# Eight rolling-cache rows to a partition on 96 and 32 neighbouring partitions, in one attention stage

## The reference, cut to what matters

```
DIL_PATTERNS = ((128, 1), (512, 4), (2048, 16))
kc = jnp.concatenate([cache_win_k[i], kb], axis=1)      # (8, 2048 + 8, 8, 64)
vc = jnp.concatenate([cache_win_v[i], vb], axis=1)
...
idx = w + arange(n_new)[:, None] - dil * arange(n_back + 1)[None, :]   # per pattern
s = einsum('bqhd,bqkhd->bhqk', q, kc[:, idx]) * scale ; softmax ; times vc[:, idx]
merge of the three patterns by their denominators
```

## Time and profile before

| | |
|---|---|
| three runs | 1942.77, 1932.91, 1943.87 us |
| profiled execution, its span | 1937.89 us, 1935.9 us |
| PE busy | 1621.9 us (84%) |
| DVE busy | 695.8 us (36%) |
| attention stage, 202 to 528 us | 326 us: PE 277.31, DVE 229.77, ACT 146.44, DMA share 0.87, 331 GB/s |
| window turns, line 1276 | 16 of them, 4.1 us of DMA waits ahead of 3 |
| window scores, line 2048 | 32.7 us busy, TensorE 11.8 us idle before it |

### The profile page before, as it was taken

The page is one execution under the profiler, slowest core; times in us unless marked ns, Lnnn a source line. Parts: engine busy times, 40 slices in busy tenths (PEclk is TensorE's granted clock), DMA queues, the critical chain, the costliest instruction groups (busy, mean ns, idle before and its releaser), DMA issues.

```text
span 1935.9 us, 32623 instructions
## 1 busy us (share of the span) xinstructions
PE 1621.9 (84%) x12772; PEld 770.8 (40%) x12772; DVE 695.8 (36%) x1351; ACT 331.3 (17%) x769; POOL 214.0 (11%) x356
## 2 busy tenths in 40 slices
PE   7999888888897978877787879998978888877784
PEld 3444455555444323222232357764532222223231
DVE  4446578867515200000000169973250000000005
ACT  3100344444302000000000020013110000000001
POOL 1000223322201110110100040000021101011000
PEclk9999999988898998999999989999979999999998
DMA  9995699989754999999999999922279999999995
GB/s 336 358 361 191 230 335 355 364 319 354 298 212 166 368 428 428 412 428 428 427 428 427 390 314 324 320 102 126 87 275 427 426 415 426 426 428 427 428 424 203
DMA packets 83829, 659.20 MB, mean 341 GB/s; under 512 B 15307, under 2 KB 15436, under 8 KB 45418
## 3 DMA queue, kind: packets, MB, share of 16 engines
q1 hardware_dynamic: 58906, 569.86, 74.0%
q0 software_dynamic: 24800, 87.65, 11.9%
HBM read 643.18 MB, written 96.53 MB: 382 GB/s over the span
## 4 chain that ended last, share of the span: by engine, by line
PE 50%; DMA 35%; DVE 9%; issue 3%; ACT 2%; SPq 1%; DVEq 0%; ACTq 0%; POOLq 0%
DMA ring<-in 32%; PE ps L2294 14%; PE ps L2249 7%; PE ps L2457 6%; PE ps L1874 6%; PE ps L1838 3%; PE ps L2063 2%; DMA ring<-y_rows 2%; PE ps L2478 2%; DVE ring L1283 2%; PE ps L2048 1%; DVE ring L1276 1%; PE ps L2314 1%; DMA out<-x 1%; PE ps L2003 1%
## 5 line engine op out<-in xcount | busy, mean ns | idle before, releaser
L2294 PE MATMUL ps<-ring,big 128*32 128x512 f32 (+1 forms) x2688 | 471.5, 649 | 135.9 <-DMA ring<-in 130.0
L2294 PEld LDWEIGHTS ps<-ring,big 128*32 128x32 f32 (+1 forms) x2688 | 146.4, 131 | 456.5 <-issue 390.1
L1555 DVE TENSOR_TENSOR big<-big,ps 128x512 f32<-128x512 f32 x32 | 22.0, 688 | 822.5 <-PE ps L2294 777.6
L2314 PE MATMUL ps<-ring,big 128*32 128x512 f32 (+1 forms) x928 | 214.0, 602 | 17.5 <-ACT big L797 12.3
L797 ACT ACTIVATE big<-ps 128x512 f32<-128x512 f32 (+6 forms) x166 | 84.3, 517 | 826.1 <-PE ps L1838 527.1
L2249 PE MATMUL ps<-ring,big 128*128 128x512 f32 (+1 forms) x288 | 123.4, 610 | 5.7 <-ACT big L1191 4.8
L2457 PE MATMUL ps<-act_t,ring 128*128 128x288 f32 x512 | 124.4, 406 | 0.0
L2314 PE MATMUL ps<-act_t,big 128*32 128x512 f32 (+1 forms) x416 | 99.0, 594 | 15.4 <-ACT big L797 10.5
L2457 PEld LDWEIGHTS ps<-act_t,ring 128*128 128x128 f32 x512 | 97.2, 190 | 26.8
L1779 DVE SCALAR_TENSOR_TENSOR big<-big,par 128x512 f32<-128x512 f32 x240 | 103.9, 510 | 0.0
L1874 PE MATMUL ps<-ring,act_t 128*128 128x512 f32 x208 | 96.9, 614 | 5.7 <-DMA ring<-in 4.4
(11 more groups left out here) (322 smaller groups left out, 1761.3 us busy)
## 6 DMA issues: line engine op xcount, KB each, us to landing
ring<-in SPq DMA_DIRECT2D x180, 2048.0 KB, 18.3
out<-in SPq DMA_DIRECT2D x16, 4080.0 KB
ring<-in SPq DMA_DIRECT2D x128, 256.0 KB, 7.0
ring<-in POOLq DMA_DIRECT2D x128, 256.0 KB, 7.3
act_t<-in SPq DMA_DIRECT2D x16, 2048.0 KB
ring<-in SPq DMA_DIRECT2D x28, 1024.0 KB, 10.2
ring<-in SPq DMA_DIRECT2D x24, 512.0 KB, 6.2
ring<-in POOLq DMA_DIRECT2D x24, 512.0 KB, 5.0
```

What stands on the lines that cost most here:

```text
L2294: ins = mm(ps[half, i, :], XgT[:, par_, k, half], slot(eslots(w)[i], 8)[:, k, :], start=(k == 0), stop=(k == KC - 1))
L2314: ins = mm(ps[half, 5 + h, :], hbT[:, k, half], down_weights(w, odd)[:, k, h * 512:(h + 1) * 512], start=(k == 0), stop=(k == 3))
```

## The change

The 1280 rows of a sequence are laid out anew. The far 768 rows go eight to a partition (16 KB in one piece, the first 8 of every 16 rows) to partitions 0 to 95. The first 256 of the last 512 rows go eight to a partition to partitions 96 to 127. The last 256 rows go two to a partition (4 KB) to all 128. So `window_far` issues two DMAs (1.5 MB to 96 partitions, 0.5 MB to 32) in place of three of 0.5 MB to 128, and `window_near` one of 0.5 MB in place of one of 1 MB. The bytes are the same. VectorE's first turn is 4096 columns wide (was 3072) and its second 1024 (was 2048). The counts that semaphores are waited for follow, and the mask table in `constants()` gives each place its new row number. Pages are loaded as before.

```diff
@@ constants()
-    far = 16 * (32 * (n // 2) + p // 4) + 2 * (p % 4) + n % 2
-    pos = np.where(n < 6, far, 1536 + 4 * p + n - 6).reshape(4, -1)
+    held = np.where(p < 96, 16 * p + n, 1536 + 8 * (p - 96) + n)
+    pos = np.where(n < 8, held, 1792 + 2 * p + n - 8).reshape(4, -1)
@@ build()
-    last_half = [None, [(kw_in[0], 48 * NB), (x_first, 16)], [None, (kw_in[1], 16 * NB)]]
+    last_half = [None, [(kw_in[0], 32 * NB), (x_first, 16)], [None, (kw_in[1], 16 * NB)]]
@@ window_far, window_near
-        far = src[b][0:1536].rearrange("(t g r e) c -> t g r (e c)", t=3, g=32, e=2)
-        for t in range(3):
-            eng.dma_start(Wkv[:, 2 * t:2 * t + 2, :], far[t][:, 0:4]).then_inc(arrived[0], 16)
+        far = src[b][0:1536].rearrange("(p r e) c -> p r (e c)", r=2, e=8)[:, 0]
+        mid = src[b][1536:1792].rearrange("(p e) c -> p (e c)", e=8)
+        for part, of in ((Wkv[0:96], far), (Wkv[96:P], mid)):
+            eng.dma_start(part[:, 0:8, :].rearrange("p n c -> p (n c)"), of).then_inc(arrived[0], 16)
-        near = src[b][1536:2048].rearrange("(p e) c -> p (e c)", p=P)
-        eng.dma_start(Wkv[:, 6:10, :], near).then_inc(arrived[1], 16)
+        near = src[b][1792:2048].rearrange("(p e) c -> p (e c)", p=P)
+        eng.dma_start(Wkv[:, 8:10, :], near).then_inc(arrived[1], 16)
@@ turn_window(b, part), VectorE
-            keys = Wkv[:, (0, 6)[part]:(6, 10)[part], :].rearrange("p n c -> p (n c)")
-            dve.wait_ge(kw_in[part], (48, 16)[part] * (b + 1))
+            keys = Wkv[:, (0, 8)[part]:(8, 10)[part], :].rearrange("p n c -> p (n c)")
+            dve.wait_ge(kw_in[part], (32, 16)[part] * (b + 1))
@@ window_products(b), TensorE
-            pe.wait_ge(vw_in[0], 64 * (b + 1))
+            pe.wait_ge(vw_in[0], 48 * (b + 1))
```

## The result

The changed kernel takes 1992.53 us (median of 4 runs, 1992.2 to 1995.24) against 1943.32 before (1932.91 to 1946.98). The ratio is 1.0268 with a 95% interval of 1.0246 to 1.0291: 52 us slower by the ratio, 49 by the medians. I had forecast 1962 and a range up to 1983.

A forecast was written before the change was run, and what follows sets the result against it. The attention stage was taken as a ring of waits, with no engine or memory full. The profiled 1937.9 us plus 22.4 us for later keys gave 1960, or 1965 on the median; forecast 1962, range 1938 to 1983.

The forecast's parts named there:

- what the stage waits for: Attention stage: a ring of waits, window turns on the path, far key load within 2 us of it every round.
- 7 s - 6.3: Key cost over seven rounds for shift s above 2.1 us, less 6.3 us slack; 22.4 us at s = 4.1.
- the whole sum: Window keys: 22.4 us of later landings, passed on in full to TensorE's idle time before the window scores.
- the turns: VectorE's window turns of 4096 and 1024 columns: about 4.5 and 1.2 us, the pair 5.6 us as before.
- the issue: Three DMAs for four on SP and POOL: counted 0; 1.8 us back if the queue limited.
- the lower bound: Far key load: nothing slows down, only the further 0.52 MB count, a shift of 1.1 us.
- the other 32 have half the data and go along beside them: Far load on 96 partitions: 64 neighbours set its time, 4.9 to 5.6 us; the other 32 add none.
- so 2.9 us cost nothing: Window values landing 2.9 us later stay within 4.7 us between last landing and products in round 6: no cost.
- I count that at nothing: Value pages 8 to 15 come 2.9 us later, when next key pages are due: counted zero, range may reach up.
- Rival B: Far load: 32 neighbours at quarter speed, shift 7.4 us, keys cost 45.5 us, time 1985 us; chance 0.17.
- Rival A: Far load: neighbours not slower, other loads fill free engines, shift 1.1 us, time 1941 us; chance 0.30.
- Rival C: Window loads: fewer, larger pieces are faster, some 2.4 us gained in the three waiting rounds; chance 0.04.

The follow-up runs named there:

- the spread form: Changed kernel with its 16 KB pieces and turns kept, rows in four loads of 32 partitions, every fourth one: 1942.80 us, ratio to before 1.0008.
- the loads alone: Program that only loads cache rows on an idle core, no kernel: 4.9 us a load for 128 partitions, 6.7 for 96 neighbours, 2.5 for the last 32.
- keys alone: Changed kernel with window values loaded the old way, only the key window the new way: 1975.78 us, ratio to before 1.0163.
- The second set of loads: Loads-only program with other partition counts and distances, and loads beside other loads: 48 neighbours 145 GB/s, 112 neighbours 284, 64 at distance 2 431.
- the pairs on one queue: Loads only: a 96-neighbour load and the load of the last 32 behind it, two such pairs on SP; a pair takes 8.9 us.
- the halves on two: Loads only: partitions 0 to 63 from SP and 64 to 127 from POOL at once, from 218.4 to some 257 us.
- three spread loads: Changed kernel with 16 KB pieces in three loads: 64 even partitions, then 32 and 32 at distance 4: 1943.09 us, ratio to before 1.0016.

## Why the prediction was wrong, point by point

**Right in the main: what the stage waits for.** Each round pays for a late landing: VectorE waited in all seven, and the spread form, whose last far key lands 1.1 us later than before in the mean, lost nothing that could be measured. With the shift that the loads alone gave, 9.2 - 3.8 = 5.4 us, my formula 7 s - 6.3 gives 31.5 us; keys alone cost 32 us. This agreement is in part luck. In the trace of keys only the last far key came 6.3 us later than before in the mean of the rounds, for which the formula gives 38 us, and VectorE's waits grew by 37.0 us. And I had expected TensorE's wait ahead of the window scores to grow by the whole sum. Its waits for VectorE grew by 19.4 us there; the rest of the stage's growth is 12.7 us of stops and 9.2 us of matmuls busy longer, neither of which my sum has.

**Right: the turns, the issue and the lower bound.** The turn pair took 5.57 us as before, and in the spread form the wait for 2.1 MB in place of 1.57 cost 3.8 us of waits and no time that could be measured.

**Wrong in size: "the other 32 have half the data and go along beside them".** 96 neighbours take 6.7 us, not 4.9 to 5.6. The last 32 took the 2.5 us that I had put down. The shift is 5.4 us alone, not 4.1, which is 7 x 1.3 = 9 us, and 6.3 us among the stage's other loads. Measured, the keys cost 32 us and not 22.4: 10 us of the miss of 30. I took the one row on neighbours for a law about halves. The second set of loads shows that no such law holds, with 48 neighbours at 145 GB/s and 112 at 284.

**Wrong in kind: "so 2.9 us cost nothing", and for the value pages "I count that at nothing".** I gave the values no cost, because 2.9 us later was within the cover of 4.7 us. They cost 15 us. The products waited only 1.4 us for the window values, so the cover held nearly as I said. I had asked only who waits for this load, not what goes on beside it: the page products waited 3.0 us for a DMA, TensorE's stops with nothing shown grew by 9.3 us, and its matmuls were busy 8.9 us longer. That the stops are loads of TensorE's instructions behind the long pieces is inferred from the packets beside them. This is the larger part of the miss. The key loads do it too: with keys only the stops are 19.0 us.

**Rival B** came nearest in size (1985, with 45.5 us for the keys, which cost 32) but not in the way: the 32 neighbours run at half speed, not a quarter, and the mean shift of 7.3 us in the whole change, near B's 7.4, is 5.4 us on an idle core. **Rival A** is refuted by the pairs on one queue and by the halves on two. **Rival C** got no support. The rule of a fixed cost for each DMA, in the Trainium skill's page DMA: Bandwidth & Descriptors ("Anatomy of one DMA — SWDGE (gpsimd) path"), would have favoured fewer loads if that cost were paid in sequence: four spread loads and three spread loads did not differ from the layout of before. The rule of ports, in the Trainium skill's page SBUF — State Buffer ("Door 1: The DMA port swizzle"), holds for 32 and 64 neighbours (210 and 211 GB/s), and the full speed of 64 partitions at distance 2 fits it as well. By the ports that it lists, 96 neighbours put at most 8 partitions on a port, as many as all 128 do, which would be 4.9 us, an estimate from that page and the 4.9 us of 128 partitions; measured are 6.7.

**Open.** Why 96 neighbours are slower than the sum over ports says is not settled, nor why 48 are slower than 32. Some 5 us between the whole change (52) and its parts (32 + 15) are within the intervals, and by the medians (49 against 34 + 16) nothing is left. TensorE's lower clock in the stage (0.86 for 0.92) goes with 15.7 us more of busy time in the same matmuls; whether it is a cause of the loss or follows from the waits, no run shows. The instruction loads were seen beside the stops in the traces; a run that takes them away was not tried.

## What to carry to other kernels

Ask of a load which partitions it covers before asking how long its pieces are: 16 KB pieces ran at full speed on 64 partitions two apart and at half or less on 32, 48 or 64 neighbours, and the repair was a stride in the destination. And ask of a slow load what shares the DMA engines with it, not only who waits for it: here value loads that came 3 us later within a cover of 4.7 us cost 15 us. Pieces of 4 KB took most of that away where the place could not be changed.

## What the hardware did that I had not expected

Two loads on two queues to the two halves of the partitions ran at 227 GB/s together, no faster than one. 48 neighbours loaded at 145 GB/s, slower than 32 (210) or 64 (211). TensorE stops in the middle of matmuls with no operand shown as missing, up to 3.9 us after the change and 2.5 us before, each time with a packet of an instruction queue in the stop or right before it. A load of 256 KB landed in 12.0 us beside a stream of 236 GB/s and in 8.0 us beside one of 425.
